# A mixture-of-experts stage in 12 slots of 128 rows in place of 13, with one expert's weights loaded twice

## The reference

```
h  = rmsnorm(x, g2)                              # 576 tokens x 1024
pg = softmax(h @ r_g)                            # 4 groups; each token takes the best
tw, ti = top_k(softmax(h @ r_e, in that group), 2)   # 2 of the 4 experts of the group
gates = (group weight x normalised tw) at the two experts
hg, hu = h @ w_gate[e], h @ w_up[e]              # 16 experts, 1024 -> 256 each
y  = sum over experts (silu(hg) * hu * gates) @ w_down[e]   # 256 -> 1024
```

## Time and profile before

| | |
|---|---|
| three runs | 957.91, 959.38, 964.58 us; median 959.38 |
| profiled execution | span 959.0 us from first to last instruction; no other time of it is given, and it lies within 0.4 us of the median |
| busy | PE 924.7 us (96%), DVE 396.8, ACT 245.8, POOL 190.9 |
| DMA | 197.51 MB, mean 206 GB/s; SP's queue, which brings the weights, 136.03 MB |
| granted TensorE clock | mean 0.989 |
| expert stages | about 310 to 467 us and 779 to 938 us |

### The profile page before, as it was taken

How to read it: one execution, slowest core, us unless ns; L and a number is a source line. 1 busy time by engine, 2 the same in 40 slices (tenths; PEclk the granted TensorE clock), 3 DMA queues, 4 the chain that set the end, 5 groups by cost and what they waited for, 6 DMA issues and landing times. The chain is left out here.

```text
span 959.0 us, 13967 instructions
## 1 busy us (share of the span) xinstructions
PE 924.7 (96%) x5140; PEld 448.3 (47%) x5140; DVE 396.8 (41%) x1007; ACT 245.8 (26%) x493; POOL 190.9 (20%) x263
## 2 busy tenths in 40 slices
PE   9999999999999999999999999999999999999991
PEld 6444445556546443334544344455564464333330
DVE  2403225667547663111333122456764774511123
ACT  3211256552111021111131113765320012211110
POOL 2233201331200111111134032023220011111100
PEclk9999999999999999999999999999999999999996
DMA  9716003351017899998772150134210279999966
GB/s 334 290 46 273 2 1 138 89 176 45 23 45 265 319 410 399 401 403 352 263 268 65 36 239 1 55 109 156 84 45 22 114 267 411 414 386 403 423 236 231
DMA packets 39197, 197.51 MB, mean 206 GB/s; under 512 B 7096, under 2 KB 7224, under 8 KB 23248
## 3 DMA queue, kind: packets, MB, share of 16 engines
q1 hardware_dynamic: 19456, 136.03, 35.7%
q0 software_dynamic: 15312, 45.72, 13.8%
q10 hardware_dynamic: 4352, 14.76, 4.3%
HBM read 176.20 MB, written 28.84 MB: 214 GB/s over the span
## 5 line engine op out<-in xcount | busy, mean ns | idle before, releaser
L715 PE MATMUL ps<-ring,hT 128*128 128x512 f32 (+3 forms) x1312 | 397.1, 584 | 1.0 <-ACT ring L1406 0.6
L715 PEld LDWEIGHTS ps<-ring,hT 128*128 128x128 f32 (+2 forms) x1312 | 150.5, 152 | 197.2 <-issue 193.6
L715 PE MATMUL ps<-ring,cat 128*128 128x512 f32 (+2 forms) x560 | 181.8, 598 | 0.0
L715 PEld LDWEIGHTS ps<-ring,cat 128*128 128x128 f32 (+2 forms) x560 | 65.7, 157 | 81.0 <-issue 79.3
L2119 DVE TENSOR_TENSOR hT<-ps,par 128x512 f32<-128x512 f32 x52 | 33.7, 686 | 154.4 <-PE ps L713 149.4
L656 POOL DMA_INDIRECT y_rows<-hn,isca x26 | 27.0, 1039 | 230.7 <-ACT hn L1484 226.9
L535 POOL TENSOR_TENSOR st<-st,half 128x1 f32<-128x1 f32 (+3 forms) x60 | 63.5, 1058 | 11.0 <-POOL st L533 10.8
L533 POOL TENSOR_SCALAR st<-st 128x1 f32<-128x1 f32 (+3 forms) x60 | 16.0, 266 | 228.8 <-DVE st L1594 83.1
L1594 DVE TENSOR_REDUCE st<-sqj 128x8 f32<-128x512 f32 x20 | 13.5, 682 | 111.5 <-ACT sqj L1318 111.4
L715 PE MATMUL ps<-hT,ring 128*128 128x512 f32 x128 | 57.1, 599 | 0.7 <-DVE tmp L1651 0.7
L1484 ACT COPY hn<-ps 128x1024 f32<-128x1024 f32 x24 | 24.3, 1012 | 95.4 <-PE ps L715 95.4
(11 more groups left out here) (278 smaller groups left out, 1136.4 us busy)
## 6 DMA issues: line engine op xcount, KB each, us to landing
ring<-in_w SPq DMA_DIRECT2D x84, 1024.0 KB, 10.7
kc<-in_w SPq DMA_DIRECT2D x10, 1024.0 KB
vc<-in_w SPq DMA_DIRECT2D x10, 1024.0 KB
v<-in_w SPq DMA_DIRECT2D x10, 1024.0 KB
kva<-in_w SPq DMA_DIRECT2D x10, 1024.0 KB
kc<-in_ck POOLq DMA_DIRECT2D x32, 256.0 KB, 3.7
vc<-in_cv POOLq DMA_DIRECT2D x32, 256.0 KB, 3.3
h_rows<-qk ACTq DMA_DIRECT2D x10, 512.0 KB, 2.6
```

The source lines that it names most:

```text
L715: ins = pe.matmul(out, lhsT, rhs, start=start, stop=stop, skip_group_check=loose)
```

## The change

There are 12 slots. From slot 3 on the positions lie otherwise in them, and the places of some change: position 2 has 128 (it had 160), 7 has 64 (96), 12 has 128 (160), 13 has 96 (128), 14 has 64 (96). A position `SPILL` = 16 is added, with 32 places in the last slot. It has no expert of its own: `spill_place` finds the first last-of-group expert that has more tokens than places, writes its number to `order[SPILL]`, and gives 32 more places to it; if there is none, expert 0 stands there with no tokens. The weights of SPILL are loaded like an expert's, so `LOADS` has 51 pieces in place of 48. The order of the first buffers (`STEADY`) begins with 4, 5, 6, 7 in place of 6, 4, 7, 8.

```diff
-W_LAYER = N_DENSE + E * PER_EXPERT
+W_ROWS = N_DENSE + E * PER_EXPERT
+SPILL = E
+W_LAYER = W_ROWS + PER_EXPERT
...
-SLOTS = [[(0, 0, 128)], [(1, 0, 128)], [(2, 0, 128)], [(4, 0, 96), (2, P, 32)], [(9, 0, 64), (10, 0, 64)], [(3, 0, 128)], [(5, 0, 96), (3, P, 32)],
-         [(6, 0, 96), (8, 0, 32)], [(7, 0, 96), (8, 32, 32)], [(11, 0, 64), (15, 0, 64)], [(13, 0, 128)], [(14, 0, 96), (12, P, 32)], [(12, 0, 128)]]
+SLOTS = [[(0, 0, 128)], [(1, 0, 128)], [(2, 0, 128)], [(3, 0, 128)], [(4, 0, 96), (3, P, 32)], [(8, 0, 64), (9, 0, 64)],
+         [(5, 0, 96), (7, 0, 32)], [(6, 0, 96), (7, 32, 32)], [(10, 0, 64), (11, 0, 64)], [(14, 0, 64), (15, 0, 64)], [(12, 0, 128)],
+         [(13, 0, 96), (SPILL, 0, 32)]]
...
-        rows_of = sb("rows_of", [P, NT, E, 4], BF16)
+        rows_of = sb("rows_of", [P, NT, E + 1, 4], BF16)
...
-        STEADY, EXTRA_BUFFERS = (6, 4, 7, 8, 5, 9, 0, 2, 1, 3), (2, 3, 6, 7, 8, 9)
+        STEADY, EXTRA_BUFFERS = (4, 5, 6, 7, 8, 9, 0, 2, 1, 3), (2, 3, 6, 7, 8, 9)
...
                             if not expert_at:
                                 sp.wait_ge(*dve_s.at("order"))
+                            if pos == SPILL:
+                                sp.wait_ge(*dve_s.at("spill"))
                             expert_at[pos] = sp.value_load(order[0:1, pos:pos + 1], min_val=0, max_val=E - 1)
...
+                def spill_place(over, cap):
+
+                    mine, before, sums = stat["spill"], stat["nov"], stat["vt"]
+                    pairs = cmpA.rearrange("p n j -> p (n j)")[:, 0:E * E].rearrange("p (a b) -> p a b", a=E)
+                    link(vec.scalar_tensor_tensor(mine, over, 0.5, c32[:, C_LAST], ALU.is_gt, ALU.mult))
+                    link(vec.tensor_tensor(pairs, across(mine, E, E), groups(c32[:, C_TRI], E, E), ALU.mult))
+                    link(vec.tensor_reduce(before, pairs, AX.X, ALU.add))
+                    link(vec.scalar_tensor_tensor(mine, before, 0.5, mine, ALU.is_lt, ALU.mult))
+                    link(vec.tensor_tensor(before, mine, c32[:, C_SLOTS][:, 16:16 + E], ALU.mult))
+                    link(vec.tensor_reduce(sums[:, 0:1], before, AX.X, ALU.add))
+                    vec.tensor_copy(order[:, SPILL:SPILL + 1], sums[:, 0:1]).then_inc(*dve_s.inc("spill"))
+                    link(vec.tensor_tensor(before, mine, cap, ALU.mult))
+                    link(vec.tensor_reduce(sums[:, 1:2], before, AX.X, ALU.add))
+                    w3 = work.rearrange("p (t e) -> p t e", t=NT)
+                    link(vec.tensor_tensor(w3, R.rearrange("p (t e) -> p t e", t=NT), across(mine, NT, E), ALU.mult))
+                    link(vec.tensor_reduce(placed_spill, w3, AX.X, ALU.add))
+                    link(vec.tensor_scalar(placed_spill, placed_spill, sums[:, 1:2], None, ALU.subtract))
+                    link(vec.scalar_tensor_tensor(cap, mine, float(LINE), cap, ALU.mult, ALU.add))
+                    link(vec.scalar_tensor_tensor(over, mine, float(-LINE), over, ALU.mult, ALU.add))
+
                 def extra_plan():
...
                     link(vec.tensor_tensor(over, stat["cnt"], cap, ALU.subtract))
+                    spill_place(over, cap)
                     link(vec.tensor_scalar(nov, over, 0.5, None, ALU.is_gt))
...
-                            ins = one_hot(s, at, placed_by[:, :, pos], first)
+                            ins = one_hot(s, at, placed_spill if pos == SPILL else placed_by[:, :, pos], first)
```

More of the change, by code:

```diff
@@ L69 @@
 C_ID, C_CAUSAL, C_BATCH, C_SPREAD, C_FIRST = (slice(i * P, (i + 1) * P) for i in range(5))
-NC32 = 8 * P + 64 + NT * 4 + 32 + E * E + 4 * E + 20
+NC32 = 8 * P + 64 + NT * 4 + 32 + E * E + 5 * E + 20
 C_TRI = slice(5 * P, 7 * P)
@@ L76 @@
 C_TIE, C_BASE, C_CAP = (slice(C_CLASS.stop + i * E, C_CLASS.stop + (i + 1) * E) for i in range(3))
-C_RANK = slice(C_CAP.stop, C_CAP.stop + E)
+C_RANK, C_LAST = (slice(C_CAP.stop + i * E, C_CAP.stop + (i + 1) * E) for i in range(2))
 C_PARTS = slice(NC32 - 20, NC32)
@@ L279, in program @@
         placed_by = o_sb[:, 1, 0:NT * E].rearrange("p (t n) -> p t n", t=NT)
+        placed_spill = o_sb[:, 1, 2 * P:2 * P + NT]
         order_of = oS[:, P:P + E * E].rearrange("p (n e) -> p n e", n=E)
@@ L284, in program @@
         both_ahead = tmp[:, 480:480 + NT * AHEAD_POS].rearrange("p (t n) -> p t n", t=NT)
-        order = sb("order", [P, E], mybir.dt.int32)
+        order = sb("order", [P, E + 1], mybir.dt.int32)
         igat = sb("igat", [P, E + EXTRA + 2], mybir.dt.uint32)
@@ L299, in program @@
                         ("mxs", 4), ("nbs", 4), ("sms", 4), ("lam", 4), ("gm", 5), ("gs", 5), ("gw", 5),
-                        ("rank", 100), ("goh", 20), ("em", 20), ("es", 20), ("ex", 80), ("ms", 8), ("rowf", 1), ("gAB", 10), ("cnt", 16), ("nov", 16), ("ovb", 16), ("vt", 5), ("size", 16), ("at", 16), ("cap", 16), ("late", 5), ("tab", 1)]:
+                        ("rank", 100), ("goh", 20), ("em", 20), ("es", 20), ("ex", 80), ("ms", 8), ("rowf", 1), ("gAB", 10), ("cnt", 16), ("nov", 16), ("ovb", 16), ("vt", 5), ("size", 16), ("at", 16), ("cap", 16), ("late", 5), ("tab", 1), ("spill", 16)]:
             stat[name] = st[:, used:used + w]
@@ L383, in program @@
         LOADS = list(dict.fromkeys(part for part, _ in USES))
-        assert len(LOADS) == E * PER_EXPERT
+        assert len(LOADS) == W_LAYER - N_DENSE
         PIECE_AT = {part: N_DENSE + j for j, part in enumerate(LOADS)}
@@ L485, in _ @@
                         sp.wait_ge(*hs_in[1].at("hs", "m", 1))
-                    at = l * W_LAYER + i
+                    at = l * W_ROWS + i
                     if i >= N_DENSE:
@@ L491, in _ @@
                                 sp.wait_ge(*dve_s.at("order"))
+                            if pos == SPILL:
+                                sp.wait_ge(*dve_s.at("spill"))
                             expert_at[pos] = sp.value_load(order[0:1, pos:pos + 1], min_val=0, max_val=E - 1)
-                        at = expert_at[pos] * PER_EXPERT + (l * W_LAYER + N_DENSE + part)
+                        at = expert_at[pos] * PER_EXPERT + (l * W_ROWS + N_DENSE + part)
                     sp.dma_start(piece(i), d["w"][bass.DynSlice(at, 1), :, :].rearrange("a p n -> (a p) n")
@@ L503, in load @@
                         sp.dma_start(piece(i),
-                                     d["w"][bass.DynSlice(l * W_LAYER + e * PER_EXPERT + (N_DENSE + j), 1), :, :].rearrange("a p n -> (a p) n")
+                                     d["w"][bass.DynSlice(l * W_ROWS + e * PER_EXPERT + (N_DENSE + j), 1), :, :].rearrange("a p n -> (a p) n")
                                      ).then_inc(*landed[SLOT[i]].inc("w", i, by=16))
@@ L1560, in constants @@
                 rows = c32[:, C_ROWS].rearrange("p (t c) -> p t c", c=4)
-                vec.tensor_copy(rows_of[:, :, :, :], rows.unsqueeze(2).to_broadcast([P, NT, E, 4]))
+                vec.tensor_copy(rows_of[:, :, :, :], rows.unsqueeze(2).to_broadcast([P, NT, E + 1, 4]))
                 vec.tensor_copy(rows_ofx[:, :, :, :], rows.unsqueeze(1).to_broadcast([P, EXTRA, NT, 4]))
@@ L1929, in by_size @@
                     link(vec.tensor_reduce(size, pairs, AX.X, ALU.add))
-                    vec.tensor_copy(order[:, :], size).then_inc(*dve_s.inc("order"))
+                    vec.tensor_copy(order[:, 0:E], size).then_inc(*dve_s.inc("order"))
                 add_out(0, 1)
@@ L2231, in layout @@
     w_in, w_out = a["w_in"], a["w_out"]
-    w = np.empty((L * W_LAYER, P, PIECE), f)
+    w = np.empty((L * W_ROWS, P, PIECE), f)
     for l in range(L):
-        parts = w[l * W_LAYER:(l + 1) * W_LAYER]
+        parts = w[l * W_ROWS:(l + 1) * W_ROWS]
         cols = blocks(w_in[l])
@@ L2279, in layout @@
     c32[:, C_RANK] = RANK_OF
+    c32[:, C_LAST] = kind
     for parts in SLOTS:
         for pos, _, wide in parts:
-            c32[:, C_CAP][:, pos] += wide
+            if pos != SPILL:
+                c32[:, C_CAP][:, pos] += wide
     rows = np.zeros((P, NT, 4))
```

## The result

| | median of its runs | against the kernel before |
|---|---|---|
| before | 959.17 to 960.52 in five sets of runs | |
| forecast | 962 (950 to 970) | within 1% |
| changed | 974.70 (971.13 to 977.48, 4 runs) | 1.0147 [1.0122, 1.0173] |

The change makes the kernel 1.5% slower, and the time lies above the forecast's range. The medians leave out one slow execution of 1067.2 us (a run of the kernel with the shorter warm-up and the filled waits, at a granted clock of 0.844). The profiled execution took 977.48 us with a span of 975.8, 16.8 more than the span of 959.0 before.

The account below looks back on a forecast made before the run. In the two expert stages, weight loads on full DMA engines and PE were taken to finish together. 959.4 + 2 x (-2.85 + 5.7 - 1.5) = 962.1, rounded 962, range 950 to 970.

Parts of the forecast that it names:

- rival A: The forecast itself: load 51 sets each expert stage's end, with the low rows' load in its way: 962; chance 0.50.
- Three loads more: In each expert stage, six loads after load 45 take about 15.2 us, and scatters in between add 1.5.
- the spread: How evenly the 16 DMA engines are loaded late in each stage: -1.5 us per stage, ends 0 and -3.0.
- The early load of the low rows: In each expert stage, y_low's load moves a slot earlier and delays the last weights: +5.7 us (bounds 0 and 5.7).
- Rival B: Load 51 sets the stage's end, but the low rows' load doesn't delay it: 951 (954 without the spread's gain); chance 0.25.
- First stage: First layer's expert stage: load 51 lands at 460.7, PE ends at 464.3 against 467.3, a gain of 3.0 us.
- Second stage: Second layer's expert stage: load 51 lands at 931.6, PE ends at 935.2 against 937.9, a gain of 2.7 us.
- Rival D: PE waits 13 us or so in each expert stage and its clock falls in the gaps: 972; chance 0.15.
- Rival C: The weights are far enough ahead in the expert stages, and PE keeps its full 24 us gain: 935; chance 0.08.
- Rival E: An expert overflows all the same and an extra slot runs, 25 us or more: 985; chance 0.02.
- overflow counts: Tokens per expert: one expert six over its 128 places in layer one, one three over 64 in layer two; no extra slot.
- Added vector work: spill_place's 14 small instructions in slot 4 take 3.5 us on DVE, covered by its idle time: cost 0.

Follow-up runs that it names:

- its control: The kernel before the change, with 15 warm-up products in place of 39 at the start of the second layer: 959.14, ratio 0.9998.
- the run with both edits: The changed kernel with 15 warm-up products in place of 39 and the wait ahead of each last down-projection filled with idle products: 964.26, ratio 1.0042.

## Why the prediction was wrong

Its mechanism, rival A, is what the stages do. What it left out lies behind them and beside them.

- *Three loads more* and *the spread* were right in their sum. Without the low rows the two terms put load 51 at 140.5 (first stage) and 142.8 us (second) after the sixth load; measured with the low rows later: 141.1 and 142.1. The pieces weren't where the forecast had them: in that run load 45 came 124.1 and 124.3 us after the sixth, earlier than the 125.3 and 127.6 that were taken from the old kernel, and the six loads behind it took 17.0 and 17.9, the 16.7 of the forecast and more, so the 1.5 that a better spread should have taken off them isn't seen. That the sum fits owes something to luck.
- *The early load of the low rows*: 5.7 forecast at the upper bound, 6.1 to 7.2 measured. The issues were at 442.6 (forecast 441 to 443) and at 928.1 (910 to 912; the whole second stage is later). Rival B is out. The rule of the Trainium skill ("DMA: Bandwidth & Descriptors", "Queues, rings and completion order"), by which queues share an engine by turns, gave the upper bound, and the trace sides with it.
- *Where it failed: the step from PE's end to the time.* "First stage" and "Second stage" take a change in the end of PE's stage as a change in the time. Behind the first stage stand a branch and a warm-up, and in the old kernel both were covered, the second only just: the branch by queued matmuls, the warm-up by the wait for the high rows (478.0 against 478.3). The forecast named no cover there and no price if it was lost. PE's late start, two next-layer loads that now fall on the branch's fetches, and a clock of half speed in the warm-up (11.68 us for what took 9.21) make it 8.0 us, by the run with a short warm-up and its control.
- *Rival D was a term, not a rival.* This is the second step that failed: the sum left the clock in PE's waits at nothing. D's condition was gaps of over 3 us ahead of the last projections, and the forecast itself had PE waiting some 13 us in each stage; it waited 14.0. D was given 0.15 as if it excluded A. The clock was at half speed twice late in each stage, as D had it (0.57 over 451 to 455 and over 912 to 916, 0.58 over 465 to 469, 0.51 over 946 to 953), behind waits of 2.4 and 4.7 us and of 2.6 and 6.2, so 3 us was no dividing line. The last down-projections took 5.3 and 6.1 us for 3.6; filling the waits ahead of them gave back 4.8 us, where D had priced 6.8 for all four.
- *Rival C*: even with the bytes of the spill taken out, a slot less on PE is worth 8.4 us and not 24.
- *Rival E and the overflow counts*: 24 scatters and no extra slot. *Added vector work*: PE ended stage 1 only 0.1 us later than before with it and 13 slots.

The terms add up: 962.1, plus 0.9 for the low rows in each stage, 8.0 and 4.8, make 976.7; less the overlap of 1.5 to 2.4 that the run with both edits showed, 974.3 to 975.2, against 974.7 measured. This closes the sum after the fact, with terms measured on the changed kernel itself.

What stays open: which of the packets of instructions each engine waited for (the trace doesn't say), whether the drop of the clock at 782 belongs to the change, and why load 45 came earlier than the forecast had it.

## What to carry to other kernels

When a stage ends later, walk on past its end: list what stands between it and the next stage (branches, warm-ups, waits), and ask of each what covers it now and by how many microseconds; a cover of 0.3 us is a term of the sum. Loads that wait for freed buffers move with the stage's end, and what they land on can cost more than the bytes did. A mechanism whose condition follows from the forecast's own numbers belongs in the sum, not beside it.

## What the runs showed of the hardware

- A branch over a long loop body that isn't run took PE's sequencer 3.3 to 4.3 us where the mean DMA share was 0.64 or less, and 4.8 to 8.7 where it was 0.79 or more, while the other engines took 0.05 to 0.07 us for theirs.
- The last three 1 MB loads of the stage landed 4 to 5 us apart with the mean DMA share down at 0.63 and 0.45, against 2.5 to 2.6 in the full stretch: the low rows and the scatters were on the engines too, and a load lands with its slowest part, for load 51 the last of 16 that were spread over 18.6 us. With the low rows out of the way the same three took 9.0 us in place of 13.9.
- In the changed kernel five waits of 2.4 to 6.2 us on PE went with stretches of 3.4 or 6.8 us at a granted clock of 0.50 (1.2 GHz); with idle products in the wait ahead of the last down-projection it stayed at 1.00 there. Not every wait did it: behind 1.50 and 1.69 us (low rows later) and behind 3.14 (no loads for the spill) the clock was 1.00.
